# A two-layer streaming encoder: six in-place slots for weight slabs, and another order at the heads of the forgetting attention

## What is computed

```python
def fox_attend(q, k, v, cq, ck, qpos, kpos):        # 8 heads of 64, "forgetting" attention
    s = jnp.einsum('bqhd,bkhd->bhqk', q, k) * FOX_SCALE
    decay = cq (per query) - ck (per key)           # cumulative log-forget values
    causal = kpos[None, :] <= qpos[:, None]
    p = jax.nn.softmax(jnp.where(causal, s + decay, NEG), axis=-1)
    return jnp.einsum('bhqk,bkhd->bqhd', p, v)

# per layer, for prompt and sample:
h = rms_norm(x, ln_mix)
o = concat(fox_attend(...), sliding_window_attend(...))      # projections from h @ w_in
x = x + o @ w_out
x = x + cross_attend(rms_norm(x, ln_mem), w_mq, mk, mv, w_mo)  # 256 memory tokens
x = x + (silu(causal_conv(gate)) * val) @ w_down               # gate, val = rms_norm(x) @ w_up
# at the end: rms_norm(x, ln_final)
```

## Time and profile before

| | |
|---|---|
| median of 3 runs | 3419.58 us (3405.64 to 3424.76) |
| the profiled execution | 3406.41 us, span 3404.6 us |
| granted TensorE clock, mean | 0.986 |
| PE busy | 95% of the span |
| DVE, POOL, ACT busy | 56%, 35%, 25% |
| DMA | 52 GB/s mean |
| chain that ended last | PE 80%, DVE 11%, ACT 5%, issue 2%, POOL 1% |

### The profile page before, as it was taken

One profiled execution on the slowest core, in us unless ns is written; L12 is line 12 of the kernel. 1 busy time (PEld: TensorE's weight loads), 2 busy tenths in 40 slices (PEclk: granted clock), 3 DMA queues, 4 the chain that ended last, 5 costly groups with the idle time before them and its releaser, 6 DMA issues.

```text
span 3404.6 us, 50260 instructions
## 1 busy us (share of the span) xinstructions
PE 3238.8 (95%) x20472; PEld 3119.4 (92%) x20472; DVE 1902.6 (56%) x3552; ACT 844.4 (25%) x1959; POOL 1208.5 (35%) x976
## 2 busy tenths in 40 slices
PE   7999999999999999999999999989899999999997
PEld 6888898888899999999988988988889999999997
DVE  6555567676744444444665655576666444444446
ACT  4432223543310000000233333144433000000002
POOL 4213222632443333334342122334425333334331
PEclk9999999999999999999999999999999999999998
DMA  4111222210111111111122112221111111111111
GB/s 158 48 54 44 57 61 69 66 44 29 37 47 45 44 44 46 42 44 47 41 78 57 45 38 64 75 70 51 47 29 41 45 46 44 44 44 47 44 44 64
DMA packets 86021, 177.57 MB, mean 52 GB/s; under 512 B 10544, under 2 KB 13872, under 8 KB 85392
## 3 DMA queue, kind: packets, MB, share of 16 engines
q1 hardware_dynamic: 71968, 132.90, 13.5%
q10 hardware_dynamic: 13824, 41.46, 4.1%
HBM read 150.36 MB, written 16.29 MB: 49 GB/s over the span
## 4 chain that ended last, share of the span: by engine, by line
PE 80%; DVE 11%; ACT 5%; issue 2%; POOL 1%; DMA 0%; DVEq 0%; SPq 0%; ACTq 0%; POOLq 0%
PE PS L606 80%; DVE ACC L1622 2%; ACT PR L1251 1%; DVE PR L1702 1%; DVE HL L1614 1%; DVE XT L1745 1%; DVE PW L1702 1%; DVE XT L1576 1%; ACT PW L1251 1%; POOL WL L588 1%; ACT PTH L1103 1%; DVE DG L1661 1%; POOL WH L586 0%; DVE PTL L1548 0%; ACT G0H L1103 0%
## 5 line engine op out<-in xcount | busy, mean ns | idle before, releaser
L586 POOL TENSOR_TENSOR WH<-RAW,zero 128x512 fp32r<-128x512 f32 x484 | 549.1, 1134 | 2110.6 <-PE PS L606 2098.3
L606 PE MATMUL PS<-HH,WH 128*128 128x384 f32 (+1 forms) x3312 | 864.8, 333 | 45.7 <-DVE HL L1614 19.2
L606 PE MATMUL PS<-HH,WL 128*128 128x384 f32 (+1 forms) x3312 | 848.2, 328 | 0.0
L606 PE MATMUL PS<-HL,WH 128*128 128x384 f32 (+1 forms) x3312 | 848.0, 328 | 0.0
L588 POOL TENSOR_TENSOR WL<-RAW,WH 128x512 fp32r<-128x512 f32 x484 | 664.4, 1373 | 38.0
L606 PEld LDWEIGHTS PS<-HH,WH 128*128 128x128 f32 x3312 | 587.1, 189 | 66.9 <-issue 23.5
L606 PEld LDWEIGHTS PS<-HL,WH 128*128 128x128 f32 x3312 | 590.0, 188 | 0.0
L606 PEld LDWEIGHTS PS<-HH,WL 128*128 128x128 f32 x3312 | 588.8, 188 | 0.0
L1745 DVE TENSOR_TENSOR XT<-PS,XT 128x320 f32<-128x320 f32 x464 | 314.2, 719 | 265.5 <-PE PS L606 265.5
L606 PE MATMUL PS<-G0H,WH 128*128 128x384 f32 (+1 forms) x960 | 274.6, 339 | 25.5 <-DVE XT L1576 16.9
L1103 ACT ACTIVATE PTH<-PS 128x512 fp32r<-128x512 f32 (+4 forms) x320 | 165.5, 520 | 518.0 <-PE PS L606 516.4
(11 more groups left out here) (252 smaller groups left out, 4716.1 us busy)
## 6 DMA issues: line engine op xcount, KB each, us to landing
RAW<-in_slabs SPq DMA_DIRECT2D x484, 256.0 KB, 2.6
XR<-decays ACTq DMA_DIRECT2D x16, 512.0 KB, 5.8
XT<-in_xT SPq DMA_DIRECT2D x8, 544.0 KB, 8.0
out_fk<-T ACTq DMA_DIRECT2D x8, 544.0 KB, 2.7
XR<-decays ACTq DMA_DIRECT2D x16, 272.0 KB, 7.1
out_fv<-T ACTq DMA_DIRECT2D x8, 544.0 KB, 3.1
out_y<-YT ACTq DMA_DIRECT2D x8, 544.0 KB, 3.1
RX<-ST ACTq DMA_DIRECT2D x24, 136.0 KB, 2.6
```

The lines of the kernel that those rows point to most:

```text
L586: pool.tensor_tensor(WH[:, s, :], RAW[:, s, :], zero[:, 0:1].to_broadcast([128, HALF]), ALU.add).then_inc(w_hi, 1)
L606: ins = pe.matmul(*a, **k)
```

## The change

It has seven pieces.

1. There are six places for slabs (`SLOTS`) in place of four, and no `RAW` of its own: `RAW` now lies over `WL`, so that POOL writes the low part over the raw data. The memory is the same, 2 x 6 in place of 3 x 4 slabs.
2. SP loads slab n when slab n-6 is released (`w_used`), no longer when the split of slab n-4 is done. POOL waits for the data alone.
3. At the start, the loads of slabs 2 and 3 stand behind the second tile of X in place of the eighth, and those of 4 and 5 behind the memory's data.
4. POOL splits slab 4 only when the normed input's eight low parts are made (`h_ready`).
5. ACT does a square of a constant first, ahead of its waits for data, and so loads its table ahead of them.
6. In steps 1 and 2 of each pair (`early`), the causal mask is added by TensorE: one more matmul per block, of the mask with the identity, into the diagonal's columns. DVE's addition falls away there.
7. In the forgetting attention, DVE takes `parts_out(s - 1, 2)` out behind the minima of step s.

```diff
--- before.py
+++ after.py
@@ -42,7 +42,7 @@
 
 FOX_SLABS = 10
 N_SLABS = 2 + PAIRS * FOX_SLABS + 8 + (4 + PAIRS * 3) + 8 + 16 + MEM_H * 3 + 8 + FT * 6 + 2
-assert N_SLABS % 4 == 0
+SLOTS = 6
 
 C_MIX, C_MEM, C_TOK, C_FFN = 0, 8, 16, 24
 C_CONV = 32
@@ -191,8 +191,10 @@
         XT = sb("XT", [128, KT, T])
         HH0 = at[0]
         HH, HL = (sb(n, [128, KT, T], F32R) for n in ("HH", "HL"))
-        RAW = sb("RAW", [128, 4, HALF])
-        WH, WL = (sb(n, [128, 4, HALF], F32R) for n in ("WH", "WL"))
+        WH = sb("WH", [128, SLOTS, HALF], F32R)
+        WL_AT = at[0]
+        WL = sb("WL", [128, SLOTS, HALF], F32R)
+        RAW = here("RAW", [128, SLOTS, HALF], F32, WL_AT)
         G0H = sb("G0H", [128, 2, T], F32R)
         G0L_AT = at[0]
         G0L = sb("G0L", [128, 2, T], F32R)
@@ -298,7 +300,7 @@
 
         x_in = [sem(f"x_in{i}") for i in range(KT)]
         ident_in, const_in, mem_in, const_ok, memset_ok = (sem(n) for n in ("ident_in", "const_in", "mem_in", "const_ok", "memset_ok"))
-        raw_in = [sem(f"raw_in{i}") for i in range(4)]
+        raw_in = [sem(f"raw_in{i}") for i in range(SLOTS)]
         w_hi, w_ready, w_used = sem("w_hi"), sem("w_ready"), sem("w_used")
         full = [sem("full0"), sem("full1")]
         free = [sem("free0"), sem("free1")]
@@ -461,6 +463,8 @@
                               outs=[(64 * h, 64, 64 * h, 64 * h, SEQ, DEC) for h in range(2)], scale=FOX_SCALE))
             with_rows(steps, G_ROWS[pair % 2])
             steps[2]["first"] = pair > 0
+            for s, st in enumerate(steps):
+                st["early"] = s <= 2
             return steps
 
         def swa_steps():
@@ -547,19 +551,22 @@
 
             def load(n):
                 l, place = divmod(n, LAYER_SLABS)
-                sp.dma_start(RAW[:, n % 4, :], slabs[l * N_SLABS + HALVES[place][1]]).then_inc(raw_in[n % 4], 16)
+                sp.dma_start(RAW[:, n % SLOTS, :], slabs[l * N_SLABS + HALVES[place][1]]).then_inc(raw_in[n % SLOTS], 16)
 
             load(0)
             load(1)
             for kt in range(KT):
                 sp.dma_start(XT[:, kt, :], xT[:, kt, :]).then_inc(x_in[kt], 16)
-            load(2)
-            load(3)
+                if kt == 1:
+                    load(2)
+                    load(3)
             for a, b in ((causal, c_causal), (tail_mask, c_tail), (FC, final_c)):
                 sp.dma_start(a[:], b).then_inc(const_in, 16)
             sp.dma_start(MR[:, :, :], memT).then_inc(mem_in, 16)
-            for n in range(4, DEPTH * LAYER_SLABS):
-                sp.wait_ge(w_ready, n - 3)
+            load(4)
+            load(5)
+            for n in range(SLOTS, DEPTH * LAYER_SLABS):
+                sp.wait_ge(w_used, n - SLOTS + 1)
                 load(n)
             for l in range(DEPTH):
                 sp.dma_start(o_tk[l], swa_tail_k[l]).then_inc(out_done, 16)
@@ -579,16 +586,16 @@
             pool.memset(one[:], 1.0).then_inc(memset_ok, 1)
 
             def split(n):
-                s = n % 4
-                pool.wait_ge(raw_in[s], (n // 4 + 1) * 16)
-                if n >= 4:
-                    pool.wait_ge(w_used, n - 3)
+                s = n % SLOTS
+                pool.wait_ge(raw_in[s], (n // SLOTS + 1) * 16)
                 pool.tensor_tensor(WH[:, s, :], RAW[:, s, :], zero[:, 0:1].to_broadcast([128, HALF]), ALU.add).then_inc(w_hi, 1)
                 pool.wait_ge(w_hi, n + 1)
                 pool.tensor_tensor(WL[:, s, :], RAW[:, s, :], WH[:, s, :].bitcast(F32), ALU.subtract).then_inc(w_ready, 1)
 
             pool.wait_ge(memset_ok, 4)
             for n in range(DEPTH * LAYER_SLABS):
+                if n == 4:
+                    pool.wait_ge(h_ready, KT)
                 split(n)
 
 
@@ -653,7 +660,7 @@
             def slab(pe, key):
 
                 assert HALVES[place.n["slab"] % LAYER_SLABS][0] == key, (key, HALVES[place.n["slab"] % LAYER_SLABS])
-                slot = place.n["slab"] % 4
+                slot = place.n["slab"] % SLOTS
                 pe.wait_ge(w_ready, place.at("slab", 1))
                 place.add("slab")
                 return slot
@@ -872,7 +879,7 @@
                     r = slice(64 * st["h"], 64 * st["h"] + 64)
                     for k, i in enumerate(st["blocks"]):
                         n, b = (i + 1) * 128, slice(i * 128, (i + 1) * 128)
-                        product(o + 512 * k, n, QH[r, b], QL[r, b], KH[r, 0:n], KL[r, 0:n])
+                        product(o + 512 * k, n, QH[r, b], QL[r, b], KH[r, 0:n], KL[r, 0:n], causal_r if st["early"] else None)
                 elif st["kind"] == "fox_s":
                     slots = slab_pair(pe, ("ck", st["pair"]))
                     for j in range(2):
@@ -1285,8 +1292,9 @@
                     act.dma_start((RX, RXB)[k][p:p + 32, :], base[w:w + 32, :]).then_inc(swap_in[k], 16)
 
             LC = [LCS[:, 0, :]]
+            act0.wait_ge(memset_ok, 4)
+            act0.activation(SM[:, 0, 0:1], one[:], ACT.Square)
             act0.wait_ge(lc_in, 16)
-            act0.wait_ge(memset_ok, 4)
             for kt in range(KT):
                 act0.wait_ge(x_in[kt], 16)
                 residual(act0, kt, LC[0][:, C_MIX:C_MIX + KT], SQ)
@@ -1666,8 +1674,9 @@
                 parts_out(-1, 1)
                 if -1 in hooks:
                     hooks[-1]()
+                ahead = steps[0]["kind"] != "fox_s"
                 for s in range(n + 3):
-                    if s:
+                    if s and ahead:
                         parts_out(s - 1, 2)
                     if s < n:
                         st = steps[s]
@@ -1681,7 +1690,7 @@
                             waits.append((p_used, place.at("step", s + 1)))
                         for produced in waits:
                             dve.wait_ge(*produced)
-                        if st["kind"] == "fox":
+                        if st["kind"] == "fox" and not st["early"]:
                             k, d = len(st["blocks"]), o + st["blocks"][0] * 128
                             diagonals = PS[:, d:d + 640 * k].rearrange("p (k n) -> p k n", n=640)[:, :, 0:128]
                             wait_own(dve, dve.tensor_tensor(diagonals, diagonals,
@@ -1705,8 +1714,8 @@
                             if half_max or j == len(st["pieces"]) - 1:
                                 ins.then_inc(sig, 1)
                         place.add("use")
-                    if s == 0:
-                        parts_out(-1, 2)
+                    if s == 0 or not ahead:
+                        parts_out(s - 1, 2)
                     if s in before:
                         before[s]()
                     if 1 <= s < n + 1:
```

## The result

The changed kernel takes 3428.88 us (median), the kernel before in the same series 3408.63; the ratio is 1.0061, 95% interval 1.0052 to 1.0070. It is slower by 20 us, where 3400 was forecast with a range to 3416. The profiled execution of the changed kernel took 3429.71 us, span 3427.9, against 3406.41 and 3404.6.

What follows compares the result with a forecast made beforehand. TensorE was taken as the bound, matmuls busy 3238.8 of 3404.6 us; only its idle time and halved clock could move. Terms summed to -16.0 us, giving 3390 (profiled) or 3403.6 (median); forecast 3400, range 3380 to 3416.

Steps and rivals of the forecast that it cites:

- Six places: Weight slabs: with six places TensorE's ten waits for POOL's split, 10.7 us, vanish; -10 us.
- rival 3: Weight slabs: the wait for POOL becomes one for the load, -10 shrinks to about 0; 3410 us, chance 0.08.
- Heads: Heads of forgetting-attention pairs 1 to 3: stall before the third transpose group falls from 1.70 to 0.6 us; -4.6 us.
- The lower clock: Behind the pair heads: with the shorter stall, full clock holds in most heads; -8 us, ends 0 and -11.4.
- Start: Kernel start: ACT's table load and slab splits moved, HL and QL end earlier; -1.6 us, ends 0 and -4.
- Boundaries: Five norm boundaries: later splits put WL ahead of QL, TensorE's wait grows by 1.05 us each; +5.3 us.
- the forecast +3.4: Norm boundaries: with waits of 2.9 us, two more falls to the lower clock; +3.4 us, ends 0 and +8.
- In the mixers there is nothing to win: Mixers: TensorE is busy 764.00 of 764.00 us at full clock, so no term was given to them.
- Rival 4: Norm boundaries: moved splits and half clock of 10.2 us at each outweigh the gains; +6, 3422 us, chance 0.06.

Runs made afterwards that it cites:

- On n-5: Changed kernel with POOL's split of slab n also waiting for the release of the slab five back: 3383.38 us, ratio 0.9927 to the kernel before.
- the hold: Changed kernel, POOL also waiting for the release five slabs back and, at the five norm boundaries, holding one slab's split until DVE has QL: 3371.81 us, ratio 0.9884.
- POOL on n-5 and the old heads: Changed kernel, POOL also waiting for the release five slabs back, without masks on TensorE and minima ahead: 3391.56 us, ratio 0.9942 to the kernel before.

## Why the prediction was wrong

**Six places: right.** Ten waits of 10.7 us were to go, and all went; no wait for a load came (rival 3 falls).

**Heads: right.** A stall of 0.6 was forecast, it is 0.65 to 0.79. The lower clock was to go behind most heads (8 us of 11.4), in the profiled execution it is gone behind all six. What the sum didn't have is that the later split alone would shorten the old stall to 1.2 us, which leaves the heads less to gain beside it. Counted from the start of the second transposes (180.51 before, 182.25 after, forecast 180.87), the chunk is out after 0.69 us, as forecast, but DG is over after 2.09 us and not 1.43, since it again ran beside WL (1.29 us).

**Start: right, then lost.** HL ends at 30.3 us (forecast 32.1), QL at 36.9 (38.2). But a new wait of 1.75 us for QLS at 62.42, where keys' and decays' steps on DVE now have a split beside them, took it back by the memory's stat (+1.4 us).

**Boundaries: right in mechanism and size.** WL comes 0.20 us ahead of QL (forecast 0.25), the wait is 3.0 to 3.1 (forecast 2.9), +6.4 us in all for +5.3. Four of five boundaries now fall to the lower clock, two did before; this was the forecast +3.4. What was left out is the additions just ahead of them: the new wait of 1.2 to 1.4 us for XT, 6.7 us in all five.

**The step that failed is the first paragraph's "In the mixers there is nothing to win".** The earlier trace rows show 764.00 of 764.00 us busy, and that was read as: nothing can happen there. It only says that nothing can be won. The change moves the 132 slab splits of a mixer by a load's length like all others, and at the boundaries the text worked out what the moved splits land on. In the mixers, where most of the splits are, it didn't. There they land on G1L and G0L, whose 64-column instructions go from 0.22 to 1.07 us, the additions behind them come late, and each of 20 pairs of turns costs 0.62 us: 12.4 us that the sum had at nothing. The same omission covers the attention and memory stages (XT +4.0, V +3.1, DG +1.0, QLS +3.3 us of waiting by the totals) and the XT additions at the boundaries (6.7 us).

In us of the profiled executions, -16.0 was forecast and +23.3 came, a gap of 39.3. The terms just named and QL's 1.1 us above forecast make up some 32 of it, if waits are added up as time. The remaining 8 us aren't broken down. The granted clock is in them, for the falls behind the heads are gone, but new ones of 3.4 us stand elsewhere (548, 562, 787, 2241 us among them), and the mean of the clock is 0.987 where it was 0.986. The runs size all that the late start costs. With the split's start put back on a release and nothing else touched, the kernel takes 3391.94 us, and that still has the 10.7 us of waits for POOL. On n-5, without them, it takes 3383.38. So all the terms of gain were there, 24 us against the 3407.18 of the kernel before beside it, and the start of the splits behind the loads cost 45.5 us, 3428.88 less 3383.38; the prediction had 8.7 us for it (5.3 and 3.4). Rival 4 had the right cause and half of the place: the boundaries' waits grew by some 13 us (QL 6.4, XT 6.7), about as much as the 12.4 of the mixers that it left out, and four of five show a fall of the clock, each of 3.4 us and not of the 10.2 that the rival needed. Since no end of any term stood for the mixers, the range ended at 3416.

At the boundaries the rule of the Trainium skill (SBUF — State Buffer, Who interferes with whom) was used: a DVE instruction with both inputs in SBUF and a GpSimd instruction that reads SBUF exclude each other whole, the first to come keeping the port. The rows here agree, those of the 64-column instructions above all, which are held for nearly the whole 1.04 us of WH. The page also says that a DVE instruction with at most one SBUF input doesn't contend outside the two-port modes, and the PSUM additions at 0.42 and 0.95 us with and without POOL agree with that. But one SBUF input alone doesn't clear an instruction: YY<-GP,LCS, a TENSOR_SCALAR with one tensor operand, takes 0.85 us with POOL idle and 1.75 beside WL. DG, which the prediction named as the row that agrees, is of this form too, and so was no test of the rule for two inputs; HL and ACC were. The rule was there; it wasn't put to all the places where it holds.

## What to carry to other kernels

A stage that is busy to the last microsecond can't win, but it can lose: where a change moves work on a side engine, lay the moved instructions against what they now run beside in every stage, the full ones first. A producer that starts on an event of the bound engine inherits its rhythm. Here POOL's splits lay on DVE's PSUM reads and on steps with time to spare, and a DMA put between event and work shifted some of them onto steps that exclude them and that TensorE waits for. How much an engine is held says little; which of its steps is held says more. Buffers that are loaded early, with the work still started by the event, keep both gains; a hold of a few splits where the other engine is on the critical path gains again.

## What the runs showed of the hardware

- An exclusion can cost a short instruction several times its length: 64 columns took 0.22 us alone and 1.07 us in the mean when a WH split had come between it and its first part.
- A TENSOR_SCALAR of DVE with a single tensor operand in SBUF and none in PSUM was held by a split as well: YY<-GP,LCS of 1090 columns took 0.85 us alone and 1.75 beside WL, DG of 128 columns 0.29 and 1.29.
- Two engines that exclude each other with instructions of like length fall into a rotation in which both run at little more than half speed: ACC additions took 1.28 us alone and 1.94 to 2.39 beside splits, which took 2.1 to 2.2 in place of 1.04 and 1.29. This was so in the kernel before, too, and was worth 12 us by the hold.
- Writing the low part over its own raw data cost at most 0.01 us an instruction in the mean (1143 and 1382 ns in place against 1134 and 1373), and 256 KB loads landed in 2.6 us as before.
- The granted clock reacts to small shifts of the waits. With the same head stalls of 1.70 us, the window of pair 2 was at 1.00 and that of pair 1 at 0.78 in the kernel before, and at 1.00 and 0.93 with POOL on n-5 and the old heads. Behind a wait of 1.8 us for QL it fell at two of five boundaries in the kernel before and at none with POOL on n-5; behind 3.0 to 3.1 us in the changed kernel it fell at four of five. A term for it needs its whole range.
